# The recurrence's gate products in rounded terms: two operands split into high and low parts, the first two pairs within the input product

## The reference, cut to what matters

```python
xc = conv(xr, conv_w) + conv_b                      # width-4 causal, one filter per channel
xh = xc.reshape(B, S, 4, 256)                       # four heads of 256 channels
gate_x = sigmoid(einsum('bshi,hij->bshj', xh, w_x) + b_x)
gate_a = sigmoid(einsum('bshi,hij->bshj', xh, w_a) + b_a)
log_a = -8 * gate_a * softplus(-a_param)
a = exp(log_a)
b = sqrt(-expm1(2 * log_a)) * (gate_x * xc)
h = associative_scan(a, b)                          # h[t] = a[t] h[t-1] + b[t]
```

## Time and profile before

| | |
|---|---|
| median of three runs | 2758.2 us |
| the profiled execution's own time | 2757.42 us |
| its span, from first to last instruction | 2755.6 us |
| PE busy | 2711.6 us, 98% of the span |
| DVE, ACT busy | 1440.7 us (52%), 1058.5 us (38%) |
| POOL busy | 36.4 us (1%) in 62 instructions |
| mean granted TensorE clock | 0.999 |
| share of PE in the chain that ended last | 91% |

### The profile page before, as it was taken

One profiled execution on the slowest core, in us unless ns is written; L12 is line 12 of the kernel. 1 busy time (PEld: TensorE's weight loads), 2 busy tenths in 40 slices (PEclk: granted clock), 3 DMA queues, 4 the chain that ended last, 5 costly groups with the idle time before them and its releaser, 6 DMA issues.

```text
span 2755.6 us, 38503 instructions
## 1 busy us (share of the span) xinstructions
PE 2711.6 (98%) x16358; PEld 2248.7 (82%) x16358; DVE 1440.7 (52%) x2360; ACT 1058.5 (38%) x1604; POOL 36.4 (1%) x62
## 2 busy tenths in 40 slices
PE   9988999999999999999999999999999999999998
PEld 7787788888887788888888888877888788888887
DVE  6834576643625756756346443274634544654433
ACT  5534454332425654433234222245433422432221
POOL 0000200000000000000000000001000000000000
PEclk9999999999999999999999999999999999999999
DMA  4200122222531002322323332236222232223222
GB/s 161 90 4 3 53 87 98 100 94 98 158 104 39 1 1 100 100 97 95 100 77 107 99 99 93 100 116 129 82 81 87 71 100 98 87 99 99 93 99 69
DMA packets 68686, 238.85 MB, mean 87 GB/s; under 512 B 7800, under 2 KB 10360, under 8 KB 68004
## 3 DMA queue, kind: packets, MB, share of 16 engines
q1 hardware_dynamic: 62256, 220.80, 23.9%
q10 hardware_dynamic: 6260, 15.59, 2.5%
HBM read 228.23 MB, written 6.03 MB: 85 GB/s over the span
## 4 chain that ended last, share of the span: by engine, by line
PE 91%; DVE 4%; ACT 3%; issue 1%; POOL 1%; DMA 0%; ACTq 0%; another core or an unknown queue 0%; DVEq 0%; POOLq 0%
PE psum L155 23%; PE psum L157 23%; PE psum L156 23%; PE psum L1330 3%; PE psum L1297 2%; PE psum L1317 2%; PE psum L843 2%; PE psum L201 2%; PE psum L202 1%; PE psum L209 1%; PE psum L1851 1%; PE psum L177 1%; PE psum L178 1%; PE psum L176 1%; PE psum L1987 1%
## 5 line engine op out<-in xcount | busy, mean ns | idle before, releaser
L155 PE MATMUL psum<-x_hi,w_hi 128*128 128x512 f32 x2128 | 846.1, 398 | 0.7 <-DVE w_lo L130 0.7
L157 PE MATMUL psum<-x_hi,w_lo 128*128 128x512 f32 x2128 | 830.4, 390 | 0.0
L156 PE MATMUL psum<-x_lo,w_hi 128*128 128x512 f32 x2128 | 829.5, 390 | 0.0
L130 DVE TENSOR_TENSOR w_lo<-raw,w_hi 128x1024 fp32r<-128x1024 f32 x409 | 500.2, 1225 | 391.7 <-ACT w_hi L123 391.6
L123 ACT ACTIVATE w_hi<-raw 128x1024 fp32r<-128x1024 f32 x409 | 427.9, 1050 | 306.0 <-DMA raw<-w_down 83.9
L155 PEld LDWEIGHTS psum<-x_hi,w_hi 128*128 128x128 f32 x2128 | 400.0, 188 | 90.6 <-issue 5.7
L156 PEld LDWEIGHTS psum<-x_lo,w_hi 128*128 128x128 f32 x2128 | 400.2, 188 | 85.5 <-issue 5.0
L157 PEld LDWEIGHTS psum<-x_hi,w_lo 128*128 128x128 f32 x2128 | 399.8, 188 | 83.8
L157 PE MATMUL psum<-h_hi,w_lo 128*128 128x512 f32 x616 | 240.0, 390 | 0.0
L156 PE MATMUL psum<-h_lo,w_hi 128*128 128x512 f32 x616 | 240.0, 390 | 0.0
L155 PE MATMUL psum<-h_hi,w_hi 128*128 128x512 f32 x616 | 240.0, 390 | 0.0
(11 more groups left out here) (412 smaller groups left out, 3298.5 us busy)
## 6 DMA issues: line engine op xcount, KB each, us to landing
raw<-w_up SPq DMA_DIRECT2D x88, 512.0 KB, 3.3
raw<-w_down SPq DMA_DIRECT2D x44, 512.0 KB, 3.3
raw<-w_f1up SPq DMA_DIRECT2D x44, 512.0 KB, 3.3
raw<-w_f2up SPq DMA_DIRECT2D x44, 512.0 KB, 3.3
raw<-w_qkv SPq DMA_DIRECT2D x36, 512.0 KB, 3.3
raw<-w_blend SPq DMA_DIRECT2D x28, 512.0 KB, 3.3
raw<-w_f1down SPq DMA_DIRECT2D x22, 512.0 KB, 3.3
raw<-w_f2down SPq DMA_DIRECT2D x22, 512.0 KB, 3.2
```

What stands on the lines that cost most here:

```text
L130: dve.tensor_tensor(self.w_lo[u % SLOTS][:], self.raw[u % SLOTS][:], self.w_hi[u % SLOTS][:].bitcast(F32), ALU.subtract).then_inc(self.lo_ ...
L155: pe.matmul(bank[:], hi, x_hi[:, kk], start=kk == 0, stop=False)
L156: pe.matmul(bank[:], hi, x_lo[:, kk], start=False, stop=False)
L157: mm = pe.matmul(bank[:], lo, x_hi[:, kk], start=False, stop=kk == kt - 1)
```

## The change

Each gate matmul in plain float32 is replaced by three in rounded terms, as in the large products. For this both operands are split. For a pair j:

- ACT rounds the pair's two weight slices of 128x512 (`round_weights`) and the pair's two tiles of `xc` (`round_input`): four copies of 128x512.
- GpSimd subtracts and gets the four low parts (`remainders`).
- PE waits for the pair's four low parts (`split_lo`) where it waited for the last tap and for the weights, and then runs 12 matmuls a gate.

Where ACT does this: for j = 0 the weights at t = 0 of the input product and the inputs at t = 2; for j = 1 the weights at t = 3 and the inputs at t = 4; each time ahead of that tile's first tap (`early`). The weights of j = 0 wait for both loads (`loaded`, 32). For j = 2 and 3 all four copies stand behind the sigmoids at h = 6 and h = 10 (`SPLITS`). GpSimd does j = 0 and 1 first, j = 2 ahead of its product of gate 3, j = 3 ahead of that of gate 5. The new tiles lie over memory that is free at that time, and no transfer is added.

```diff
@@ lru_input, act
         for t in range(KD):
             k.act_ahead(act, g, t)
             k.tile_kept(act, g, t)
+            early(act, t)
             act.activation(mem.xc[:, t], k.sq[t % 2][:], ACT.Identity, bias=k.v("lconv_b", t),
                            scale=k.v("lconv_w3", t)).then_inc(first, 1)
@@ Scan
+    def round_weights(self, act, j):
+        mem, (_, _, wh) = self.mem, self.operands(j)
+        if j == 0:
+            act.wait_ge(mem.loaded, 32)
+        if j >= 2:
+            act.wait_ge(self.pair, 2 * j - 2)
+        for hi, w in zip(wh, (mem.wx, mem.wa)):
+            act.activation(hi, w[:, 4 * P * j:4 * P * (j + 1)], ACT.Copy).then_inc(self.w_high, 1)
+
+    def round_input(self, act, j):
+        mem, (xh, _, _) = self.mem, self.operands(j)
+        if j == KD // 2 - 1:
+            act.wait_ge(self.made, 2)
+        act.wait_ge(self.tap3, 2 * j + 2)
+        for kt in range(2):
+            act.activation(xh[kt], mem.xc[:, 2 * j + kt], ACT.Copy).then_inc(self.x_high, 1)
+
+    def remainders(self, pool, j):
+        mem, (xh, xl, wh) = self.mem, self.operands(j)
+        c = slice(4 * P * j, 4 * P * (j + 1))
+        for m, (hi, w, lo) in enumerate(zip(wh, (mem.wx, mem.wa), (mem.wx_lo, mem.wa_lo))):
+            pool.wait_ge(self.w_high, 2 * j + m + 1)
+            pool.tensor_tensor(lo[:, c], w[:, c], hi.bitcast(F32), ALU.subtract).then_inc(self.split_lo, 1)
+        for kt in range(2):
+            pool.wait_ge(self.x_high, 2 * j + kt + 1)
+            pool.tensor_tensor(xl[kt], mem.xc[:, 2 * j + kt], xh[kt].bitcast(F32), ALU.subtract).then_inc(self.split_lo, 1)
+
+    def early(self, act, t):
+        if t in (0, 3):
+            self.round_weights(act, t // 3)
+        if t in (2, 4):
+            self.round_input(act, t // 2 - 1)
@@ Scan.pe
             if t == 0:
-                pe.wait_ge(mem.loaded, 32)
                 k.tile_kept(pe, self.source, 5)
...
-            pe.wait_ge(self.tap3, t // 2 * 2 + 2)
-            for bank, w in zip(self.gate_banks(t), (mem.wx, mem.wa)):
+            j = t // 2
+            xh, xl, wh = self.operands(j)
+            pe.wait_ge(self.split_lo, 4 * j + 4)
+            for bank, hi, w in zip(self.gate_banks(t), wh, (mem.wx_lo, mem.wa_lo)):
                 for kt in range(2):
-                    o = ((t // 2 * 2 + kt) * 2 + t % 2) * P
-                    mm = pe.matmul(bank, w[:, o:o + P], mem.xc[:, t // 2 * 2 + kt], start=kt == 0, stop=kt == 1)
+                    c = slice((kt * 2 + t % 2) * P, (kt * 2 + t % 2 + 1) * P)
+                    low = w[:, 4 * P * j:4 * P * (j + 1)][:, c]
+                    pe.matmul(bank, hi[:, c], xh[kt], start=kt == 0, stop=False)
+                    pe.matmul(bank, hi[:, c], xl[kt], start=False, stop=False)
+                    mm = pe.matmul(bank, low, xh[kt], start=False, stop=kt == 1)
@@ Scan.act
+        if h in SPLITS:
+            self.round_weights(act, 2 + SPLITS.index(h))
+            self.round_input(act, 2 + SPLITS.index(h))
@@ Scan.pool
+        self.remainders(pool, 0)
+        self.remainders(pool, 1)
         for t in range(KD):
+            if t in (3, 5):
+                self.remainders(pool, (t + 1) // 2)
             pool.wait_ge(self.gx, t + 1)
```

More of the change, by code:

```diff
@@ L1755, with lru_input @@
 REL_TILE = 6
-def lru_input(k, name, mem, sem, norm):
+def lru_input(k, name, mem, sem, norm, early):
     g = Product(k, name, plain(KD, KD, k.x_hi, k.x_lo), range(BANKS))
@@ L1812, in lru_input @@
     return g
+SPLITS = (6, 10)
 class Scan:
@@ L1827, in __init__, with operands @@
         self.ones = sem("dl_ones")
+        self.w_high, self.x_high, self.split_lo = sem("lru_w_high"), sem("lru_x_high"), sem("lru_split_lo")
+    def operands(self, j):
+        k, mem = self.k, self.mem
+        r, e = k.rounded, mem.e_rounded
+        ga, gx = mem.ga_rounded, mem.gx_rounded
+        if j % 2 == 0:
+            return [ga[:, KD - 2], gx[:, KD - 2]], [ga[:, KD - 1], gx[:, KD - 1]], (r[:, 4], r[:, 5])
+        if j == 1:
+            return [ga[:, KD - 4], gx[:, KD - 4]], [ga[:, KD - 3], gx[:, KD - 3]], (r[:, 6], mem.z_rounded[:, 8])
+        return [e[:, 4], e[:, 5]], [r[:, 2], r[:, 3]], (r[:, 6], mem.z_rounded[:, 8])
+    def round_weights(self, act, j):
[27 more added lines that the diff above has]
+            self.round_input(act, t // 2 - 1)
     def gate(self, h):
@@ L2290, in build @@
         k.w_hi = [sb(f"w_hi{j}", [P, UB * P], F32R) for j in range(SLOTS)]
+        with ExitStack() as s:
+            k.rounded = sb("sq_to_r_rounded", [P, 7, T], F32R, s)
         k.sq = [sb(f"sq{j}", [P, T]) for j in range(2)]
@@ L2348, in build @@
                 B.rec_lo = sb("rec_lo", [P, KD, T], F32R, s2)
+            with ExitStack() as s2:
+                B.ga_rounded = sb("lru_ga_rounded", [P, KD, T], F32R, s2)
             B.ga = sb("lru_ga", [P, KD, T], stack=s)
@@ L2355, in build @@
                     ("pick", [32, SKEW]), ("mask", [12, SKEW]), ("rv", [12, SKEW]), ("table", [32, 12])))
+            with ExitStack() as s2:
+                B.e_rounded = sb("lru_e_rounded", [P, KD, T], F32R, s2)
             B.e = sb("lru_e", [P, KD, T], stack=s)
@@ L2360, in build @@
                 last = [sb(f"dil_last{j}", [P, T], stack=s2) for j in range(7)]
+            with ExitStack() as s2:
+                B.z_rounded = sb("z2_even_rounded", [P, 9, T], F32R, s2)
             z_even = sb("z2_even", [P, 9, T], stack=s)
@@ L2371, in build @@
                 B.xc = sb("lru_xc", [P, KD, T], stack=s2)
+                with ExitStack() as s3:
+                    B.wx_lo, B.wa_lo = sb("lru_wx_lo", [P, 2 * D], F32R, s3), sb("lru_wa_lo", [P, 2 * D], F32R, s3)
                 B.wx, B.wa = sb("lru_wx", [P, 2 * D], stack=s2), sb("lru_wa", [P, 2 * D], stack=s2)
         with ExitStack() as s:
+            with ExitStack() as s2:
+                B.gx_rounded = sb("lru_gx_rounded", [P, KD, T], F32R, s2)
             B.gx = sb("lru_gx", [P, KD, T], stack=s)
@@ L2466, in build @@
         k.phases.append(Phase(act=load_lru))
-        xr = lru_input(k, "xr", B, sem, norm)
+        xr = lru_input(k, "xr", B, sem, norm, lambda act, t: scan.early(act, t))
         scan = Scan(k, B, xr, dram, sem)
```

## The result

| | before | after |
|---|---|---|
| median (lowest to highest) | 2757.94 us (2757.53 to 2758.71), 4 runs | 2777.07 us (2775.68 to 2778.45), 4 runs |
| ratio, 95% interval | | 1.0070 (1.0057 to 1.0083) |
| profiled execution | 2757.42 us, span 2755.6 | 2778.22 us, span 2776.4 |
| mean granted clock | 0.999 | 0.995 |

A forecast was written before the change was run, and what follows sets the result against it. TensorE, fed by ACT and DVE's loop without slack, was the bound. Terms 12.3 + 3.2 + 4.8 = 20.3 us gave +19.8 at host 1; less 5.0 for gates, plus 4 at gate 6: 18.8, hence 2777 us; range 2768 to 2786.

The forecast's parts named there:

- What bounds the kernel: Input product: TensorE busy 98%, fed by an ACT and DVE loop without slack, so delay passes on nearly one for one.
- host 1: Host tile between gates 0 and 1 on TensorE; DVE frees its bank 0.5 us ahead; forecast to start 19.8 us later.
- Xr 6: Input-product tile on TensorE; first matmul forecast near 1844, with 12 us of idle time ahead of it.
- Gates: Eight gates on TensorE: 12 rounded matmuls take 2.72 us against 3.44, saving 0.72 us a gate.
- The weights' wait: At t = 0, ACT's first tap waits for the load of `wa` and two copies: 12.3 us later.
- Copies: At t = 2, 3 and 4, ACT's copy pairs ahead of the tap delay DVE's loop: 3 x 1.1 = 3.2 us.
- Turns: GpSimd's subtractions and DVE's taps exclude each other, one collision in each of four input-product places: 4 x 1.2 = 4.8 us.
- Rival B: Input product and gate 6: no turns with GpSimd and no wait at gate 6; +10.0 us, 2768; chance 0.14 with nearby outcomes.
- Gate 6: TensorE waits there for pair 3's low parts, late behind ACT's transfer wait: 4 us, range 0 to 8.
- Rival C: TensorE's clock falls behind its waits at xr 6 and gate 6; one tile more, 5.45 us: +24.3, 2782.5; chance 0.18.
- no slack: Later stretches: none seen there to take back the delay; the forecast is wrong if they do.

The follow-up runs named there:

- pair 3 earlier: The changed kernel with pair 3 rounded at h = 8 instead of 10, its subtractions one place sooner on GpSimd: 2776.42 us, ratio 1.0071.
- the wait moved: The changed kernel with pair 3 at h = 8 and ACT's wait for the 3.8 MB write ahead of h = 16's third exponential group: 2776.68 us.
- two pairs later: Against the changed kernel, only pairs 2 and 3 split, at h = 6 and 8; pairs 0 and 1 in plain float32: 2757.22 us, ratio 1.0000.

## Why the prediction was right, point by point

- **What bounds the kernel.** ACT and DVE's loop in the input product, with 0.5 us to spare at host 1. The delay reached TensorE nearly whole: +20.3 at `sq` of xr 6, +19.9 at host 1 (forecast 20.3 and 19.8). Both hold the 0.5 us that the trace was late beforehand. Xr 6 itself started at 1845.3 and not near 1844, because the collision at xr 0 stands ahead of its weights too.
- **Gates.** 0.72 us each was forecast, 0.73 measured.
- **The weights' wait.** 12.3 forecast, 12.9 measured. That it cost 12.4 us of time alone is no second measurement of this term: there 11.2 us of delay became 10.3 of waiting and 2.7 of lower clock.
- **Copies.** 3.2 forecast, 3 x 1.04 = 3.1 measured.
- **Turns.** 4.8 forecast, 3.9 measured: four groups longer by 1.15, 0.89, 0.91 and 0.91. One meeting a place was assumed and seen; its price was 0.9 to 1.15 instead of 1.2. Without these subtractions all four were back at 2.32. Rival B, no turns, is out.
- **Gate 6.** 4 forecast, 4.5 of waiting measured (4.7 from start to start), from the cause given: ACT's `w_hi` waited for its transfer until 1905.29 (forecast 1904.9), the low parts were ready at 1922.4 (forecast 1922.4).
- **Rival C, the clock.** It fell, to 0.50 behind xr 6's wait, where DVE set the pace and nothing was lost, and behind gate 6's for a shorter time, where it cost 1.5 us, not the 5.45 of a whole tile. The forecast's sum holds nothing for it; that was too little, and the 2.7 us in the run with the wait alone show that the first fall was hidden only by the other delays.
- **Where it was luck.** The profiled execution should have taken 2776.2 us and took 2778.2: gate 1 came 0.3 later, gate 6 another 0.7, its clock cost 1.5, the gates gave back 0.1 more, and 0.3 came back at the end. Up to gate 1 the misses nearly cancel: the weights' wait 0.6 too small, the turns 0.9 and the copies 0.1 too large, and 0.5 that the trace was late beforehand. That run is the second longest of the four, and their median, 1.1 us lower, fell on the forecast.
- **What was missing.** The forecast added gate 6's wait as if it could be taken out alone, and saw "no slack" in the later stretches. There is a second limit at nearly the same place: the write of 3.8 MB, 54.5 to 56 us from issue to the point where ACT is let go, and the weight loads beside it. While gate 6 waited, that limit was hidden behind it. Three expectations of the experiments failed on it (pair 3 earlier, with and without the wait moved; two pairs later), the middle one also on the clock in host 1. In the kernel before, ACT's 0.28 us of idle time in front of the table load was the sign of it.

What stays open: what decides whether the clock falls in host 1, behind waits that are alike; whether a GpSimd instruction that only writes holds up the taps; and whether pair 0 can be had in rounded terms at all without loss, since no version with four pairs came below before.

## What to carry to other kernels

In a loop of two engines that hand tiles to each other without slack, a small instruction costs its whole length if it stands ahead of the handoff, and behind it only what it sets off elsewhere (here 4.2 us of copies, of which 1.3 came back as longer collisions); a wait for a load there costs what is left until the load *lands*, so look up the landing of every load that a moved step needs, not its issue. GpSimd's free time isn't free for DVE: count one collision for each subtraction that can meet a DVE instruction with two SBUF inputs. Before you promise a wait's length as a gain, look for the next thing that ends near it: a long transfer whose waiter idles only tenths of a microsecond is a limit, and it doesn't move when the compute ahead of it gets shorter. And to every wait that a change puts on TensorE belongs the question whether the clock falls behind it and whether TensorE sets the pace there; if it does, count the fall as a term of its own.

## What the runs showed of the hardware

- During a wait of 13.1 us on TensorE the granted clock fell to 0.50; the work behind it ran at that level for some 5 us. Behind a wait of 4.5 us the clock averaged 0.70 over 5 us, and 12 matmuls of 128x512 took 4.16 us instead of 2.72. Behind one of 10.3 us a tile of 24 took 8.2 us instead of 5.45.
- Shorter waits had it both ways. Behind 1.7 us at gate 0 and 1.9 to 2.7 at host 1 the clock fell in two of five executions (0.67 and 0.69 from 1870 to 1875, 1.6 us lost) and stayed at 1.00 in three; behind a single wait of 1.0 us it was 0.71 from 1825 to 1830.
- A group of three DVE taps of 2.32 us together took 3.2 to 3.5 us where one GpSimd subtraction met it, and up to 4.87 where more did.
- The write of 3.8 MB held its waiter until 54.5 to 56 us after its issue, with weight loads beside it. A weight load of 512 KB beside it took up to 19.7 us in the kernel before, where the shortest of the same stretch took 3.1.
